# Two 64-row tiles or four: state-space products of a fused two-block kernel, regrouped on TensorE

## What is computed

```python
def _s5(u, lam_re, lam_im, log_dt, b_re, b_im, c_re, c_im, d_skip, w_glu, b_glu):
    ug = u.reshape(bsz, seq, N_SSM_GROUPS, SSM_GROUP)         # 32 groups of 16 channels, 64 states each
    ...
    bu_re = jnp.einsum("blgh,gph->blgp", ug, bb_re)
    bu_im = jnp.einsum("blgh,gph->blgp", ug, bb_im)
    ...
    _, _, s_re, s_im = lax.associative_scan(combine, (a_re_t, a_im_t, bu_re, bu_im), axis=1)
    y = (jnp.einsum("blgp,ghp->blgh", s_re, c_re) - jnp.einsum("blgp,ghp->blgh", s_im, c_im) + d_skip * ug)
    z = jax.nn.gelu(y.reshape(bsz, seq, D_SSM))
    return z * jax.nn.sigmoid(z @ w_glu + b_glu)
```

## Time and profile before

| | us |
|---|---|
| median of three runs | 1764.43 (1763.96 to 1764.52) |
| the profiled execution | 1764.34 |
| its span, first to last instruction | 1762.8 |
| PE busy in the span | 1743.5 (99%) |
| the state-space and attention stretch, first `chunk_inputs` to last `glu` of it | 1283.47 to about 1339 |

### The profile page before, as it was taken

The page is one execution under the profiler, slowest core; times in us unless marked ns, Lnnn a source line. Parts: engine busy times, 40 slices in busy tenths (PEclk is TensorE's granted clock), DMA queues, the critical chain, the costliest instruction groups (busy, mean ns, idle before and its releaser), DMA issues.

```text
span 1762.8 us, 23781 instructions
## 1 busy us (share of the span) xinstructions
PE 1743.5 (99%) x8970; PEld 1428.0 (81%) x8970; DVE 1058.1 (60%) x1585; ACT 739.7 (42%) x1047; POOL 175.0 (10%) x231
## 2 busy tenths in 40 slices
PE   8999999999999999999999999999999999999998
PEld 7888888888888677888788788888977888888887
DVE  6666437555563666755788853447596665555433
ACT  5322222333444886623333322225575455555321
POOL 2222001220000000004411120120001300000000
PEclk9999999999999999999999999999999999999999
DMA  8777422343222211123655562225131223232232
GB/s 261 231 225 225 137 74 82 116 140 96 96 73 94 72 49 63 58 96 121 208 179 143 151 173 78 94 93 193 45 145 49 96 96 96 97 99 88 84 102 77
DMA packets 171715, 206.89 MB, mean 117 GB/s; under 512 B 18420, under 2 KB 150130, under 8 KB 171122
## 3 DMA queue, kind: packets, MB, share of 16 engines
q1 hardware_dynamic: 145010, 161.97, 28.4%
q0 software_dynamic: 12640, 38.55, 6.9%
q10 hardware_dynamic: 13984, 5.27, 1.4%
HBM read 190.29 MB, written 17.56 MB: 118 GB/s over the span
## 4 chain that ended last, share of the span: by engine, by line
PE 93%; DVE 3%; ACT 2%; issue 1%; DMA 1%; ACTq 0%; SPq 0%; DVEq 0%
PE bank L2231 39%; PE bank L2170 35%; PE bank L2506 6%; PE bank L2532 1%; PE bank L2630 1%; PE bank L2138 1%; DVE w_lo L1283 1%; DMA w_raw<-in_ffn_w_up 1%; PE bank L2400 1%; PE bank L2884 1%; ACT w_hi L724 1%; PE bank L2543 1%; PE bank L2598 0%; PE bank L2896 0%; PE bank L2254 0%
## 5 line engine op out<-in xcount | busy, mean ns | idle before, releaser
L724 ACT CAST w_hi<-w_raw 128x2048 fp32r<-128x2048 f32 x156 | 297.9, 1909 | 729.6 <-PE bank L2231 352.2
L1283 DVE TENSOR_TENSOR w_lo<-w_raw,w_hi 128x2048 fp32r<-128x2048 f32 x158 | 367.2, 2324 | 351.5 <-ACT w_hi L724 350.9
L2231 PE MATMUL bank<-h_hi,w_hi 128*128 128x512 f32 x1024 | 400.9, 391 | 0.5 <-DVE h_lo L1324 0.2
L2231 PE MATMUL bank<-h_hi,w_lo 128*128 128x512 f32 x1024 | 398.8, 389 | 0.0
L2231 PE MATMUL bank<-h_lo,w_hi 128*128 128x512 f32 x1024 | 315.5, 389 | 0.0
L2231 PEld LDWEIGHTS bank<-h_hi,w_hi 128*128 128x128 f32 x1024 | 192.2, 188 | 44.8 <-issue 3.2
L2231 PEld LDWEIGHTS bank<-h_lo,w_hi 128*128 128x128 f32 x1024 | 192.3, 188 | 40.1
L2231 PEld LDWEIGHTS bank<-h_hi,w_lo 128*128 128x128 f32 x1024 | 192.3, 188 | 39.3
L2170 PE MATMUL bank<-hid_hi,w_hi 128*128 128x512 f32 (+1 forms) x538 | 207.6, 386 | 0.0
L2170 PE MATMUL bank<-hid_lo,w_hi 128*128 128x512 f32 (+1 forms) x538 | 207.3, 385 | 0.0
L2170 PE MATMUL bank<-hid_hi,w_lo 128*128 128x512 f32 (+1 forms) x538 | 207.2, 385 | 0.0
(11 more groups left out here) (490 smaller groups left out, 2521.3 us busy)
## 6 DMA issues: line engine op xcount, KB each, us to landing
w_raw<-in_w_in SPq DMA_DIRECT2D x29, 1024.0 KB, 5.1
mod_raw<-in_w_mod POOLq DMA_DIRECT2D x96, 256.0 KB, 4.8
w_raw<-in_ffn_w_up SPq DMA_DIRECT2D x22, 1024.0 KB, 5.5
w_raw<-in_w_up SPq DMA_DIRECT2D x22, 1024.0 KB, 5.1
w_raw<-in_ffn_w_gate SPq DMA_DIRECT2D x21, 1024.0 KB, 5.4
w_raw<-in_ffn_w_down SPq DMA_DIRECT2D x16, 768.0 KB, 4.5
w_raw<-in_ffn_w_down SPq DMA_DIRECT2D x16, 640.0 KB, 4.0
w_raw<-in_w_out SPq DMA_DIRECT2D x8, 1024.0 KB, 5.3
```

Of the source, the lines that this page charges most:

```text
L724: act.copy(w_hi[i % 2][:], w_raw[i % 2][:]).then_inc(S("w_hi_done"), 1)
L1283: dve.tensor_tensor(w_lo[s][:], w_raw[s][:], w_hi[s][:].bitcast(F32), ALU.subtract).then_inc(S("w_split"), 1)
L2231: mm = pe.matmul(bank[:], w[:, k, at], h[:, k, :], start=k == first and part == 0 and i == 0, stop=k == last and part == 1)
```

## The change

The arrays of state tiles are laid out anew. Within a half, the second quarter's two groups of each tile exchange their place: what was in partitions 0 to 63 is in 64 to 127 and the other way round. This is done where the tables are fetched (the source in DRAM is unchanged) and where ACT copies the turned inputs' source `u2t`. The results of the second quarter then go to the result partitions where they always were, so `t=0` of the first quarter uses array rows 0 to 63 and result partitions 0 to 63, and `t=0` of the second quarter uses rows 0 to 63 and result partitions 64 to 127. `chunk_inputs` and `within_chunks` take a tile of each quarter in turn, in this way in four 64x64 parts of the array. `chunk_inputs` runs in two passes, with a wait for the first pass (`bu`) before the second. `within_chunks` is now called per half.

```diff
-            sp.dma_start(wb[:], wb_dram[:]).then_inc(S("w0_tables_landed"), 16)
+            wb_to, wb_from = (tile[:].rearrange("p (w q s) i l c -> p w q (s i l c)", w=2, q=2) for tile in (wb, wb_dram))
+            sp.dma_start(wb_to[:, :, 0], wb_from[:, :, 0]).then_inc(S("w0_tables_landed"), 16)
+            for rows in range(2):
+                sp.dma_start(wb_to[64 * rows:64 * rows + 64, :, 1],
+                             wb_from[64 - 64 * rows:P - 64 * rows, :, 1]).then_inc(S("w0_tables_landed"), 16)
...
-                for t in range(2):
-                    act.copy(u2t[:, :, t, b, :].rearrange("p (k j) h -> p k j h", k=4),
-                             u2_bank(b)[:].rearrange("p (k t j h) -> p t k j h", k=4, t=2, j=4)[:, t]).then_inc(S("u2_out"), 1)
+                for rows, blocks in ((0, slice(0, 4, 3)), (1, slice(1, 3))):
+                    act.copy(u2t[:, :, rows, b, :].rearrange("p (w q j) h -> p w q j h", w=2, q=2),
+                             u2_bank(b)[:].rearrange("p (w x j h) -> p w x j h", w=2, x=4, j=4)[:, :, blocks]).then_inc(S("u2_out"), 1)
...
             sw_max(4)
             sw_max(5)
-            split(PART["glu"][0])
             chunks(0, (4, 5))
             chunks(1)
             sw_max(6)
             sw_max(7)
+            split(PART["glu"][0])
             z_split((0, 1))
+            sw_scale(6)
+            sw_scale(7)
             dve.wait_ge(S("sw_out"), 6)
             dve.tensor_tensor(yat_sq[:, :, 0:3 * P], ...)
-            sw_scale(6)
-            sw_scale(7)
             sw_last()
...
-                for s in range(NS // 2):
-                    st = NS // 2 * half + s
-                    for part in range(2):
+                for first_part in range(2):
+                    if first_part:
+                        pe.wait_ge(S("bu"), 2 * half + 1)
+                    for s in range(QUAD):
                         for late in range(2):
                             for t in range(2):
-                                own = slice(64 * t, 64 * t + 64)
-                                mm = pe.matmul(input_bank(half, part)[own, s * NC:(s + 1) * NC], wb[own, st, part, late, :],
-                                               uc[own, st, late, :], start=late == 0, stop=late == 1)
-                mm.then_inc(S("bu"), 1)
+                                own, other = slice(64 * t, 64 * t + 64), slice(64 - 64 * t, P - 64 * t)
+                                for j, part, rows in ((s, first_part, own), (QUAD + s, 1 - first_part, other)):
+                                    st = NS // 2 * half + j
+                                    mm = pe.matmul(input_bank(half, part)[rows, j * NC:(j + 1) * NC], wb[own, st, part, late, :],
+                                                   uc[own, st, late, :], start=late == 0, stop=late == 1)
+                    mm.then_inc(S("bu"), 1)
...
+                            for q, rows in ((2 * half, own), (2 * half + 1, other)):
+                                mm = pe.matmul(chunk_bank(q)[rows, j * P + later:(j + 1) * P], uc[own, QUAD * q + j, late, :],
+                                               tz[own, QUAD * q + j, late, later:], start=j == 0 and late == 0, stop=False)
+                mm.then_inc(S("bu"), 1)
...
+                pe.wait_ge(S("bu"), 5 + q // 2)
```

More of the change, by code:

```diff
@@ L1941, in chunks @@
                 t = [scan_t[:, i] for i in range(4)]
[L1942 removed]
+                dve.wait_ge(S("bu"), 2 * half + 2)
                 if half == 0:
[L1944 removed]
+                    dve.wait_ge(S("w0_tables_landed"), 80)
                     done(dve.memset(state[:, :, :, 0:1], 0.0))
@@ L2738, in within_chunks @@
                         for t in range(2):
-                            own = slice(64 * t, 64 * t + 64)
+                            own, other = slice(64 * t, 64 * t + 64), slice(64 - 64 * t, P - 64 * t)
                             later = P // 2 * late
-                            pe.matmul(chunk_bank(q)[own, j * P + later:(j + 1) * P], uc[own, QUAD * q + j, late, :], tz[own, QUAD * q + j, late, later:],
-                                      start=j == 0 and late == 0, stop=False)
+                            for q, rows in ((2 * half, own), (2 * half + 1, other)):
+                                mm = pe.matmul(chunk_bank(q)[rows, j * P + later:(j + 1) * P], uc[own, QUAD * q + j, late, :],
+                                               tz[own, QUAD * q + j, late, later:], start=j == 0 and late == 0, stop=False)
+                mm.then_inc(S("bu"), 1)
             def from_states(q):
@@ L2819, in _ @@
             chunk_turn(3)
+            chunk_inputs(1)
             within_chunks(0)
-            chunk_inputs(1)
-            within_chunks(1)
             sw_turn(4)
@@ L2828, in _ @@
             sw_scores(7)
-            within_chunks(2)
+            within_chunks(1)
             turn_back(0)
@@ L2832, in _ @@
             turn_back(1)
-            within_chunks(3)
             sw_values(5)
```

20 lines of the change are left out of this document (10 added, 10 removed).

## The result

| | median of its runs | of before, measured beside it | ratio, 95% interval | profiled execution, its span |
|---|---|---|---|---|
| the changed kernel | 1769.80 (1768.54 to 1772.00, 6 runs) | 1764.27 (1763.96 to 1764.69, 6 runs) | 1.0033 [1.0023, 1.0043] | 1770.68, 1769.2 |

The change costs 5.5 us where the prediction had a gain of 1.4 and a range up to 1765.8. It is slower, by 0.3%, and the forecast is wrong by 6.8 us.

A forecast was written before the change was run, and what follows sets the result against it. The prediction took PE's own work as the bound, busy 1743.5 of 1762.8 us (99%). The profiled 1764.34 less a gain of 1.4 at `glu(0)` gave 1762.9, the median 0.1 above: 1763.0, range 1762.0 to 1765.8.

The forecast's parts named there:

- Step 10: Tables fetched in three pieces: four more issues on SyncE at 0.34 us; cost 0, at most 0.5; `tz` 0.
- the key panel is late by 0.5: Rival: key panel late by 0.5 us, total 1763.4; chance 0.13 shared with a late pause or rounds in between.
- Steps 1 and 4: First `chunk_inputs` takes 2.4 us for 3.95; `within_chunks(0)` of both quarters takes 1.35 us, a single quarter took 1.39.
- the first rival: Four array parts run no faster, `chunk_inputs` takes 3.9 us, no gain: 1764.4, between 1763.8 and 1765.0; chance 0.25.
- Step 2: DVE's start of `chunks(0)`: without the gate panel's low part ahead, it begins at 1286.1, 2.0 us earlier.
- step 3: Second `chunk_inputs` waits for ACT's quarter 3 copies, not made earlier; begins 1290.35 for 1290.72, first one's gain becomes waiting.
- Step 5: PE's pause for instructions comes earlier, about 1292.9, until 1295 to 1297; `from_states(0)` could begin at 1298.0 to 1300.
- Steps 7 and 8: PE ends `from_states(3)` at 1313.1 to 1315, then waits for DVE's gate low part; `glu(0)` at 1316.2, gain 1.4 us.
- Step 9: Behind the start of `glu(0)`, turns and scaling follow PE's list; all later work shifts by the same 1.4 us.
- The clock rival: PE idle up to 3.1 us ahead of `glu(0)` lowers the clock, losing 2 to 4 us: 1765 to 1767; chance 0.07.

The follow-up runs named there:

- h1: The kernel before, with its one transfer of table `wb` made two, one of the even and one of the odd rows: 1763.56 us.
- e4: The changed kernel with `wb` and `tz` both stored with rows already exchanged and each fetched in one transfer: 1764.09 us.
- e1: The changed kernel with the key panel loaded ahead of the tables `wb` and `rotc`, not behind them: 1762.29 us.
- e3: The changed kernel with `wb` stored already exchanged and fetched in one transfer, `tz` still in three pieces: 1764.77 us.
- g1: f4 with sixteen matmuls of no use added, six around the last `chunk_turn` and ten ahead of `glu(0)`: 1762.77 us.
- g2: f4 with only six matmuls of no use added, around the last `chunk_turn`: 1764.35 us.
- f2: e4 with the gate panel's low part put back ahead of the first `chunks`: 1764.18 us.
- f4: e4 with the key panel loaded ahead of table `wb`: 1763.65 us.
- e2: The kernel before, with `wb` fetched in three pieces shaped as in the change, but no rows exchanged: 1769.77 us.
- f3: e1 with the load of the first `w_out` panel held back until `from_states(0)` has ended: 1769.30 us.
- g4: The kernel before, with `wb` fetched by two transfers, rows 0 to 63 and rows 64 to 127: 1771.66 us.
- g3: The kernel before, with the key panel loaded ahead of its two tables and nothing else changed: 1764.31 us.

## Why the prediction was wrong

- **Step 10 failed, and with it the forecast.** It priced the tables in pieces at "Cost 0, at most 0.5": four issues of 0.34 us and "the same bytes in smaller runs". It took each of the two further issues of `wb` at 0.34 us and the bytes' time as unchanged. The three issues took 1.89 us, from `1209.84 0.64` and `1210.52 1.25`, where the sum had 1.02, which is no more than a part of it (h1's two issues took 1.15 and cost nothing). The term that was wrong is the bytes' time: a transfer over the upper or lower 64 rows takes packets of 1.16 us for 0.64, and while the pieces were in flight all queues together moved 241 GB/s for 383. The slack of 0.65 us was rightly read from the earlier trace rows, but PE was held up for 4.49 us, and 2.14 more were lost behind it, nearly all by the low clock. The rival "the key panel is late by 0.5" had the right mechanism and a ninth of its size. With this loss gone the forecast gain still isn't shown: e4 takes 1764.09, inside the stated range and level with before.
- **The same step said 0 for `tz`.** It looked at when the table is used and not at what else its slow packets delay. They lengthen the pause: 2.96 to 3.24 us with `tz` in pieces (after, e1, e3), 1.09 to 1.72 with it in one (g1, g2, f2), where the execution's clock or the fillings differ too. The instruction packet ahead of the pause goes 10.8 us behind the first `chunk_inputs` in the changed kernel and 8.4 behind it in e4.
- **Steps 1 and 4, the matmuls, were right.** `chunk_inputs` takes 2.41 us for a predicted 2.4. The rows of L2308 decided rightly against the first rival, and 64 columns of weights in place of 16 don't lengthen the round. `within_chunks` of two quarters takes 1.57 us for 1.35 in e4, 0.2 more than its rounds gave.
- **Step 2 was right, and step 3 nearly.** L1955 begins 2.66 us behind the start of the first `chunk_inputs`, for 2.63. The gain of the first `chunk_inputs` does become waiting, 1.13 us ahead of the last `chunk_turn` and 0.72 behind it. But "Nothing in the change makes ACT earlier there" was wrong by 0.4 us: before, ACT had itself waited 0.44 us for PE's `sw_values(3)`, a wait that goes when PE is earlier. The second `chunk_inputs` begins at +6.49 for +6.88.
- **Step 5, the pause**, came where it was expected (1299.14, that is 1293.65 with the shift of 5.49 taken off, for 1292.9) and ended at the late end of its range. A second one, 0.67 us in `chunk_inputs(1)`, wasn't foreseen. In the kernels with one transfer each (e4, f2, f4, g1, g2) `chunk_inputs(1)` has none.
- **Steps 7 and 8 were right in size where their conditions held**: +32.7 was the sum, +32.79 is e4, with PE idle 3.13 us for the predicted "up to 3.1". In the changed kernel itself they did not come about, because PE was late by the pause and the clock: `glu(0)` at +34.47.
- **Step 9** holds where PE idles ahead of `glu(0)` and the clock stays at 1.00: from there to the norm's sums f4 takes 12.25 us, before 12.30. In the changed kernel it takes 12.79, and PE waits 0.24 us in it for ACT's `oc`.
- **The clock rival had 0.07** and was real: after, e1, e2, e3, e4, f2, f3, f4 and g4 each have a stretch at the low clock, between 1233 and 1320, at changing places. Its rate was right (half as fast at the low level; at the program's start, from which it was read, the profile gives the clock as 1.00, so only the doubled times spoke for it there), its chance was not. I had argued from the one pause of 1.71 us in the earlier trace rows that idle time so short has no effect; in the changed kernel PE's idle time came in a row of 1.13, 0.72, 0.67 and 3.24 us within 9.4 us, and in e4 and f4 the first two were enough.

## What to carry to other kernels

- A transfer's price is not its bytes alone: ask which rows it covers, and let each transfer cover both halves of the tile's rows. If one half must be fetched by itself, put it behind everything that somebody is about to wait for, or lay the data out as needed when they are written.
- Where a step adds DMAs, follow each panel queued behind them to its first reader, and compare the slack with the transfer's whole time at half its rate, not with the cost of the issue. Then ask the same of each instruction that stands behind the reader's wait.
- A gain of 1 us in a stretch in which PE idles 3 us is not safe: the idle time can cost the clock, and that takes back more.

## What the hardware did that I had not expected

- Four 64x64 parts run side by side at 64 moving columns. A pass of 64 matmuls takes (2.41 - 0.15)/2 = 1.13 us by the prediction's split, (1.13 - 0.22)/15 = 61 ns for a round of four, 15 ns for each matmul. The single starts in the trace say the same: 58 to 59 ns from one round of four to the next, as for a round of two before. The 25 ns that the Trainium skill gives as the least distance of two starts ("TensorE: Matmul & The Clock Gate", section "Wait — 56ns, not 53.3ns?") doesn't hold for matmuls on different parts of the array.
- The same idle time cost the clock in one execution and not in another: it fell behind PE's 3.13 us ahead of `glu(0)` in e4, and stayed at 1.00 behind 3.14 in f4 and 3.13 in g2. Nor does it need the change: PE waits 1.58 us for ACT's `h_hi` near 1395 in before and in g3, and the clock from 1396 to 1400 is 1.00 in the one and 0.57 in the other. A stretch at the low clock cost 1.3 us (f4's `chunk_inputs(1)` against g1's) to 2.0 (after's key products). No row tells which way it goes.
- PE runs out of instructions although it has no branch here: pauses of 0.7 to 3.2 us, longest with the pieces of `tz` in flight and shorter with less data. They appear as "issue" in the chain, and the long one of each kernel ends 2.2 to 2.6 us behind the start of a packet of the instruction queue. That the packet is what PE waits for is inferred from this; no row names the releaser.
